# Second softmax of each head's pair in PSUM, and the first block's norms and lambda's steps rearranged

## The chip, the cores and the metric

The kernel runs on one core of one Trainium2 chip. The metric is the device time of one execution in microseconds (us). The engines are TensorE (PE), VectorE (DVE), ScalarE (ACT), GpSimd (POOL) and SyncE (SP), which here only issues DMAs and opens the layers.

## The reference

256 tokens of width 1024 pass through two layers of a first block and then two layers of a second block, all in fp32. The change touches the first block alone:

```python
h = rms_norm(x, attn_norm_g[l])
proj = h @ w_in[l]
rq, rk, rv, rg, dq, dk, dv = jnp.split(proj, split_at, axis=-1)
ret = retention_bidir(rq, rk * RET_HEAD_DIM ** -0.5, rv, lg_f, lg_b)       # 8 heads of 64
ret = rms_norm(ret, ret_norm_g[l]) * jax.nn.silu(rg)
dqn = rms_norm(dq, dq_norm_g[l]) * DIFF_HEAD_DIM ** -0.5                   # 4 heads, each a pair of 64
dkn = rms_norm(dk, dk_norm_g[l])
lam = exp(sum(lambda_q1 * lambda_k1)) - exp(sum(lambda_q2 * lambda_k2)) + lam_init
da = diff_attention(dqn, dkn, dv, lam, slopes)     # (softmax(one) - lam * softmax(two)) @ v, with ALiBi
da = rms_norm(da, diff_norm_g[l]) * (1.0 - lam_init)
x = x + concatenate([ret, da]) @ w_out[l]
h = rms_norm(x, ffn_norm_g[l])
x = x + (silu(h @ w_gate[l]) * (h @ w_up[l])) @ w_down[l]
```

The second block (convolutions, two attentions, and a feed-forward that gathers rows of a table by indirect DMA) takes some 1700 of the 2400 us and is left as it is.

## The kernel before

Tokens lie on the 128 partitions in two tiles, t = 0 and 1 (`TT` = 2). `x_res` holds the residual stream, `xn` its normed rows, and the normed rows are transposed by TensorE into four PSUM banks and then split into `hT_hi` (ScalarE, L1302) and `hT_lo` (VectorE, L1659). Every weight goes the same way: SyncE loads chunks of 128 x 1024 into three slots of `raw`, ScalarE rounds each to its high part (L1279), GpSimd subtracts to make the low part (`low_part`, L1153), and TensorE multiplies three times per product (high by high, high by low, low by high; L629 is the helper that issues every matmul). There are six slots for the split pairs. Twenty-eight chunks are used up to the attention part, eight by the out projection, and 66 by the feed-forward. Each engine runs a program in an order written out by hand, and semaphores tie them together.

A layer of the first block, as far as it matters here:

- **Start.** The layer is opened by SyncE. VectorE's `norm_x` squares and sums both tiles (L1703), lets ScalarE take both roots at once (`root`, L1265), takes the reciprocals (L1706) and scales both tiles (L1709). Behind that VectorE makes lambda's two products (L1723) and two gains (L1725, L1726), and only then `hT_lo` from the transposed rows. After it come lambda's two sums (L1731, L1733) and the exponents of retention's decays (L1738 to L1741). ScalarE empties the transposed rows, takes exps of the decays' parameters and of lambda, and then exps of `rel`, with the high parts of weights in between.
- **Groups.** TensorE makes `dq` in acc[0], acc[1] and `dk` in acc[2], acc[3] (`acc` are the first four PSUM banks; the other four rotate by a plan). ScalarE squares them, VectorE reduces (L1749), ScalarE takes the root, and VectorE writes the normed groups `dqk` (L1755, L1761). TensorE waits for `dqk_ready` between its third and its fourth pair of feature blocks, to transpose two heads (L769).
- **Attention.** Scores k = 2h and 2h + 1 are the pair of head h. `biased(k)` adds ALiBi and takes the row maxima (L1770, L1775), ScalarE's `exps(k)` works in place (L1385), and `difference(h)` takes reciprocals (L1780), times lambda (L1782), scales the second softmax (L1785) and subtracts it from the first (L1789). All of this lies in `prob`, four slots in SBUF, and `attn(h, t)`. VectorE's order is biased 0 to 3, difference 0 and 1, biased 4 to 7, decayed(0), difference(2), decayed(1), difference(3), decayed(2), decayed(3), where `decayed(p)` multiplies two heads' retention scores by the decays (L1804). TensorE makes `dv`, then `ret_out(0)`, scores, `ret_out(1)`, scores, and `ret_out(2)`, which waits for `decayed(2)`. Behind that it transposes `attn`, multiplies with `dv`, transposes `mix` (L861) and runs the out projection.
- **Before the feed-forward.** The projection comes out of TensorE in the order half 0 (tile 0, tile 1), half 1 (tile 0, tile 1), each announced by `out_full`. VectorE adds a half when both its tiles are there (L1846), and after the second half runs `norm_x` as at the start.

## Time and profile before

| | |
|---|---|
| three runs, median | 2408.61 us |
| three runs, lowest and highest | 2403.22 and 2413.67 us |
| the profiled execution | 2408.13 us, with a span of 2406.3 us |
| granted TensorE clock, mean over the span | 0.944 of full |
| busy, share of the span | PE 82%, DVE 65%, POOL 52%, ACT 28% |
| chain that ended last, by engine | DMA 38%, PE 36%, DVE 17%, issue 4%, ACT 2%, POOL 2% |
| the first block's two layers | 0 to 356 us, 358 to 706 us |

The chain follows the last instruction back to what released it, step by step, so its shares say who held the end, and busy shares do not. The DMA share is the second block's gathers. In the first block the chain is nearly all TensorE's and VectorE's.

### The profile page before, as it was taken

What the parts mean: (1) busy time and instruction counts of PE and PEld (TensorE: products, weight loads), DVE (VectorE), ACT (ScalarE), POOL (GpSimd) and SP (SyncE); (2) the same over time, 40 slices, a digit from 0 to 9 for tenths busy, and PEclk for the clock granted to TensorE, in tenths of its full rate; (3) what the DMA queues carried; (4) which work ended last, traced back from release to release, by engine and by line L of the source; (5) the groups of instructions that cost most, each with busy time, mean ns of one, the idle gap of its engine ahead of it and who ended that gap; (6) DMA issues with size and microseconds to landing.
All of it is one profiled execution on the core that took longest, in us unless ns stands there. A gap on an engine that the chain in (4) does not pass through costs nothing.

```text
span 2406.3 us, 25784 instructions
## 1 busy us (share of the span) xinstructions
PE 1978.0 (82%) x8464; PEld 1303.1 (54%) x8464; DVE 1569.0 (65%) x3650; ACT 666.9 (28%) x1231; POOL 1246.8 (52%) x828
## 2 busy tenths in 40 slices
PE   7989999989998669888777777797688887777776
PEld 6779988779987555443232222386544433232232
DVE  7732126641115759888788877666498987888776
ACT  5534436544435421211011110154221111010100
POOL 7738867648872146555444444130455554444441
PEclk9989998999999779999999999997799999999999
DMA  5425544426554159999999999651499999999996
GB/s 177 159 70 195 192 153 159 140 96 201 183 193 147 62 193 396 421 419 421 421 421 421 421 421 421 271 191 61 154 399 421 420 421 421 421 422 420 421 420 275
DMA packets 118012, 700.21 MB, mean 291 GB/s; under 512 B 13968, under 2 KB 13968, under 8 KB 51856
## 3 DMA queue, kind: packets, MB, share of 16 engines
q0 software_dynamic: 73728, 536.90, 53.9%
q1 hardware_dynamic: 44176, 161.96, 19.7%
q8 instruction: 56, 0.92, 0.2%
q14 instruction: 52, 0.43, 0.1%
HBM read 697.76 MB, written 1.05 MB: 290 GB/s over the span
## 4 chain that ended last, share of the span: by engine, by line
DMA 38%; PE 36%; DVE 17%; issue 4%; ACT 2%; POOL 2%; SPq 0%; DVEq 0%; POOLq 0%; ACTq 0%
PE ps L629 35%; DMA arena<-in_table,arena 18%; DMA late_row<-in_table,arena 18%; DVE arena L2203 3%; POOL w_split L1153 2%; DVE late_row L2203 1%; DVE diag L2213 1%; DMA row_sb<-in_table,arena 1%; DVE arena L1925 1%; DVE arena L1789 1%; DVE arena L1785 1%; ACT arena L1471 1%; POOL arena L1239 1%; ACT w_split L1279 1%; DVE arena L1723 0%
## 5 line engine op out<-in xcount | busy, mean ns | idle before, releaser
L1153 POOL TENSOR_TENSOR w_split<-raw,w_split 128x1024 fp32r<-128x1024 f32 x260 | 636.5, 2469 | 399.4 <-ACT w_split L1279 397.6
L629 PE MATMUL ps<-late_row,diag 128*128 128x512 f32 x1000 | 472.0, 615 | 120.4 <-DVE diag L2213 120.4
L629 PE MATMUL ps<-arena,diag 128*128 128x512 f32 x888 | 431.6, 630 | 133.3 <-DVE diag L2213 133.3
L629 PE MATMUL ps<-hT_hi,w_split 128*128 128x256 f32 x2624 | 503.4, 290 | 28.5 <-POOL w_split L1153 23.9
L629 PEld LDWEIGHTS ps<-hT_hi,w_split 128*128 128x128 f32 x2624 | 419.6, 193 | 38.6 <-issue 27.2
L1239 POOL DMA_INDIRECT late_row<-in_table,arena x250 | 285.2, 1141 | 298.1 <-PE ps L629 277.9
L1239 POOL DMA_INDIRECT arena<-in_table,arena x222 | 253.0, 1140 | 324.7 <-PE ps L629 268.4
L629 PEld LDWEIGHTS ps<-late_row,diag 128*128 128x128 f32 x1000 | 185.8, 194 | 396.6 <-DVE diag L2213 206.5
L629 PE MATMUL ps<-hT_lo,w_split 128*128 128x256 f32 x1312 | 374.4, 285 | 0.0
L629 PEld LDWEIGHTS ps<-arena,diag 128*128 128x128 f32 x888 | 167.5, 198 | 380.1 <-DVE diag L2213 210.1
L2203 DVE CUSTOM_DVE_ANT_0 late_row<-late_row,x_res 128x1024 f32<-128x1024 f32 x250 | 307.4, 1235 | 98.1 <-DMA late_row<-in_table,arena 98.1
L1565 ACT ACTIVATE arena<-arena 128x2 f32<-128x2 f32 x260 | 52.9, 203 | 1120.6 <-DVE arena L2203 1120.6
L1279 ACT ACTIVATE w_split<-raw 128x1024 fp32r<-128x1024 f32 x288 | 300.6, 1057 | 195.9 <-DMA raw<-in_stream 140.5
L2203 DVE CUSTOM_DVE_ANT_0 arena<-arena,x_res 128x1024 f32<-128x1024 f32 x222 | 277.0, 1254 | 90.6 <-DMA arena<-in_table,arena 90.1
L629 PEld LDWEIGHTS ps<-hT_lo,w_split 128*128 128x128 f32 x1312 | 253.8, 193 | 7.2 <-issue 5.3
L629 PE MATMUL ps<-w_split,hT_hi 128*128 128x512 f32 x640 | 211.7, 414 | 20.5 <-DVE hT_lo L1659 6.0
L1673 DVE TENSOR_TENSOR arena<-arena,ps 128x256 f32<-128x256 f32 x44 | 18.6, 422 | 290.9 <-ACT arena L1329 290.9
L2213 DVE TENSOR_SCALAR diag<-ident,arena 128x128 f32<-128x128 f32 x512 | 175.3, 400 | 22.6 <-ACT arena L1565 16.3
L629 PEld LDWEIGHTS ps<-w_split,hT_hi 128*128 128x128 f32 x640 | 125.7, 200 | 52.0 <-issue 11.8
L629 PE MATMUL ps<-w_split,hT_lo 128*128 128x512 f32 x320 | 130.0, 406 | 0.0
L629 PE MATMUL ps<-arena 128*128 128x64 f32 (+7 forms) x632 | 108.6, 354 | 24.5 <-ACT arena L1313 13.0
L629 PEld LDWEIGHTS ps<-arena 128*128 128x128 f32 (+2 forms) x632 | 94.1, 227 | 41.6 <-ACT arena L1313 15.2
(241 smaller groups left out, 1914.9 us busy)
## 6 DMA issues: line engine op xcount, KB each, us to landing
raw<-in_stream SPq DMA_DIRECT2D x288, 512.0 KB, 3.3
row_sb<-in_row SPq DMA_DIRECT2D x2, 2306.5 KB, 11.2
late_row<-in_table,arena POOLq DMA_INDIRECT x250, 30.1
arena<-in_table,arena POOLq DMA_INDIRECT x222, 29.1
arena<-in_sub SPq DMA_DIRECT2D x2, 1024.0 KB, 11.5
arena<-in_small SPq DMA_DIRECT2D x2, 640.0 KB, 8.8
x_res<-in_x SPq DMA_DIRECT2D x1, 1024.0 KB, 5.7
out_x<-x_res SPq DMA_DIRECT2D x2, 512.0 KB, 5.3
```

The lines of the kernel that those rows point to most:

```text
L629: ins = nc.tensor.matmul(o, lhsT, rhs, start=start, stop=stop)
L1153: pool.tensor_tensor(w_lo[pair], raw[:, at % raws, :], w_hi[pair].bitcast(F32), ALU.subtract).then_inc(lo_ready, 1)
L1239: pool.indirect_dma_start(out=slots[slot_of[n]], out_offset=None, in_=table, in_offset=bass.IndirectOffsetOnAxis(ap=picked[:, u, at:at + 1 ...
L1279: A(w_hi[pair_of(c, self.pairs, self.narrow)], raw[:, slot, :], ACT.Copy).then_inc(hi_ready, 1)
L1471: ins = A(prob2[:, k % 4, t, 0:n], prob2[:, k % 4, t, 0:n], ACT.Exp, bias=negmax2[:, k, t:t + 1], accum_out=sums2[:, k, t:t + 1])
L1565: A(acts[:, some], dots[:, some], ACT.Gelu).then_inc(acts_ready, 1)
L1673: V.tensor_tensor(full, value, gate, ALU.mult).then_inc(gate_step, 1)
L1785: step(V.tensor_scalar(attn(h, t), prob[:, two % 4, t, :], rsum[:, two, t:t + 1], None, ALU.mult))
L1789: V.scalar_tensor_tensor(out=attn(h, t), in0=prob[:, one % 4, t, :], scalar=rsum[:, one, t:t + 1], in1=attn(h, t), op0=ALU.mult, op1=ALU.s ...
L1925: step(V.scalar_tensor_tensor(out=dst[:, c, :], in0=x, scalar=tap, in1=dst[:, c, :], op0=ALU.mult, op1=ALU.add))
L2203: ins = V.tensor_tensor_reduce(out=x, in0=x, in1=x_res[:, n // TILE_ROWS, :], scale=1.0, scalar=0.0, op0=ALU.mult, op1=ALU.add, accum_out= ...
L2213: V.tensor_scalar(diag[:, n % DIAGS, :], ident[:], acts[:, n:n + 1], gate[:, n // TOP, n % TOP:n % TOP + 1], ALU.mult, ALU.mult).then_inc( ...
```

## The change

1. `probs(k)` stands where `prob[:, k % 4]` stood: for odd k, the second softmax of each pair, it is a PSUM bank, acc[2] for heads 0 and 2 and acc[3] for heads 1 and 3. Bias, exp, scaling and difference of odd k read and write it there, and `attn(h, t)` is written only by the last step.
2. At a layer's start tile 0's sum of squares is ScalarE's and tile 1's is VectorE's, and each tile has its own root, reciprocal and scaling.
3. Lambda's products and the two gains stand behind the decays' exponents on VectorE, lambda's exp behind the decays' exp on ScalarE, and lambda's sums behind `dqk`.
4. Before the feed-forward each tile of each half is added as it comes. The squares of half 0 are summed in advance and go, scaled and with epsilon, into the bias of the root (`eps_x`), tile 0's half 1 is squared by VectorE and tile 1's by ScalarE, and each tile has its own root.
5. ScalarE tries a root of a constant (`root_tried`) ahead of each layer's opening. Counts of `std_ready` are renumbered.

```diff
+        def probs(k):
+            return acc[2 + k // 2 % 2].rearrange("p (t c) -> p t c", t=TT) if k % 2 else prob[:, k % 4]
...
-                root(1, std_x, ss_x, 1.0 / D, eps1)
+                A(xn[:, 0, :], x_res[:, 0, :], ACT.Square, accum_out=ss_x[:, 0:1]).then_inc(act_step, 1)
+                act.wait_ge(act_step, 1)
+                root(None, std_x[:, 0:1], ss_x[:, 0:1], 1.0 / D, eps1)
+                root(1, std_x[:, 1:2], ss_x[:, 1:2], 1.0 / D, eps1)
                 w.upto(0)
                 act.wait_ge(par_ready, 32)
                 empty_transposed(B, w, "xT", col1_sb[:, 0:DT])
                 A(dece, row1_sb[:, slice(*r1["dec"])], ACT.Exp).then_inc(dec_ready, 1)
-                act.wait_ge(lam_ready, 1)
-                A(lam_e, lam_s, ACT.Exp).then_inc(lame_ready, 1)
...
                 A(decay[:, :, P:2 * P], decay[:, :, P:2 * P], ACT.Exp).then_inc(decay_ready, 1)
+                act.wait_ge(lam_ready, 1)
+                A(lam_e, lam_s, ACT.Exp).then_inc(lame_ready, 1)
...
-                        ins = A(prob[:, k % 4, m, :], prob[:, k % 4, m, :], ACT.Exp, bias=negmax[:, k, m:m + 1],
+                        ins = A(probs(k)[:, m, :], probs(k)[:, m, :], ACT.Exp, bias=negmax[:, k, m:m + 1],
...
-                root(4, std_x, ss_x, 1.0 / D, eps1)
+                act.wait_ge(ms_ready, 4)
+                A(std_x[:, 0:1], ss_x[:, 0:1], ACT.Sqrt, bias=eps_x[:, 0:1], scale=1.0 / D).then_inc(std_ready, 1)
+                act.wait_ge(ms_ready, 5)
+                A(xn[:, 1, 512:D], x_res[:, 1, 512:D], ACT.Square, accum_out=ss_x[:, 1:2]).then_inc(act_step, 1)
+                act.wait_ge(act_step, 3)
+                A(std_x[:, 1:2], ss_x[:, 1:2], ACT.Sqrt, bias=eps_x[:, 1:2], scale=1.0 / D).then_inc(std_ready, 1)
...
                 with act.Fori(0, DEPTH) as l:
+                    if n == 1:
+                        A(root_tried, eps1[:, 0:1], ACT.Sqrt)
                     enter_layer(act, "act", l + n)
...
+            def sum_of_squares(t, c, out):
+
+                x = x_res[:, t, c]
+                return V.tensor_tensor_reduce(out=xn[:, t, c], in0=x, in1=x, scale=1.0, scalar=0.0,
+                                              op0=ALU.mult, op1=ALU.add, accum_out=out)
+
+            def normed_rows(step, t, n):
+
+                dve.wait_ge(std_ready, n)
+                step(V.reciprocal(rstd_x[:, t:t + 1], std_x[:, t:t + 1]))
+                step.settle()
+                V.tensor_scalar(xn[:, t, :], x_res[:, t, :], rstd_x[:, t:t + 1], None, ALU.mult).then_inc(rows_ready, 1)
...
-                norm_x(step, 1)
-                dve.wait_ge(par_ready, 32)
...
+                step(sum_of_squares(1, slice(0, D), ss_x[:, 1:2]))
+                step.settle()
+                dve.sem_inc(ms_ready, 1)
+                for t in range(TT):
+                    normed_rows(step, t, t + 1)
                 empty_transposed(B, "xT", col1_sb[:, 0:DT])
-                dve.wait_ge(lame_ready, 1)
-                step(V.tensor_tensor(lam_d, lam_e[:, 0:1], lam_e[:, 1:2], ALU.subtract))
-                step.settle()
-                step(V.tensor_tensor(lam, lam_d, par("lam_init"), ALU.add))
...
                 dve.sem_inc(dist_ready, 1)
 
+                dve.wait_ge(par_ready, 32)
+                lq, lk = par("lq"), par("lk")
+                for m in range(2):
+                    c = slice(64 * m, 64 * m + 64)
+                    step(V.tensor_tensor_reduce(out=falling[:, 0, c], in0=lq[:, c], in1=lk[:, c], scale=1.0, scalar=0.0,
+                                                op0=ALU.mult, op1=ALU.add, accum_out=lam_s[:, m:m + 1]))
+                step(V.tensor_scalar(gq, par("dq_g"), 64 ** -0.5, None, ALU.mult))
+                step(V.tensor_scalar(gd, par("diff_g"), par("out_scale"), None, ALU.mult))
+                step.settle()
+                dve.sem_inc(lam_ready, 1)
...
                 ins.then_inc(dqk_ready, 1)
+
+                dve.wait_ge(lame_ready, 1)
+                step(V.tensor_tensor(lam_d, lam_e[:, 0:1], lam_e[:, 1:2], ALU.subtract))
+                step.settle()
+                step(V.tensor_tensor(lam, lam_d, par("lam_init"), ALU.add))
...
-                        ins = V.tensor_tensor_reduce(out=prob[:, k % 4, t, :], in0=b[:, t * SEQ:(t + 1) * SEQ],
+                        ins = V.tensor_tensor_reduce(out=probs(k)[:, t, :], in0=b[:, t * SEQ:(t + 1) * SEQ],
...
-                        step(V.tensor_scalar(attn(h, t), prob[:, two % 4, t, :], rsum[:, two, t:t + 1], None,
+                        step(V.tensor_scalar(probs(two)[:, t, :], probs(two)[:, t, :], rsum[:, two, t:t + 1], None,
                                              ALU.mult))
                     step.settle()
                     for t in range(TT):
-                        V.scalar_tensor_tensor(out=attn(h, t), in0=prob[:, one % 4, t, :],
-                                               scalar=rsum[:, one, t:t + 1], in1=attn(h, t),
+                        V.scalar_tensor_tensor(out=attn(h, t), in0=probs(one)[:, t, :],
+                                               scalar=rsum[:, one, t:t + 1], in1=probs(two)[:, t, :],
                                                op0=ALU.mult, op1=ALU.subtract).then_inc(attn_ready, 1)
...
+                def added(t, c):
+                    dve.wait_ge(out_full, 3 + TT * c + t)
+                    x = x_res[:, t, halves[c]]
+                    step(V.tensor_tensor(x, x, acc[2 * t + c], ALU.add))
+
+                for t in range(TT):
+                    added(t, 0)
+                step.settle()
+                for t in range(TT):
+                    step(sum_of_squares(t, halves[0], ss_x[:, t:t + 1]))
+                step.settle()
+                step(V.tensor_scalar(eps_x, ss_x, 1.0 / D, float(EPS1), ALU.mult, ALU.add))
+                step.settle()
+                added(0, 1)
+                step.settle()
+                step(sum_of_squares(0, halves[1], ss_x[:, 0:1]))
+                step.settle()
+                dve.sem_inc(ms_ready, 1)
+                added(1, 1)
+                step.settle()
+                dve.sem_inc(ms_ready, 1)
+                for t in range(TT):
+                    normed_rows(step, t, 6 + t)
```

## Rows read from the trace of the kernel before

**Rows 1.** Stage, first layer's attention: length; busy PE, PEld, DVE, ACT, POOL; PEclk; DMA

```profile
94.00:136.00 42.00, 36.02 (x200) 31.32 (x198) 31.08 (x51) 19.05 (x38) 22.04 (x10) 0.84 0.32 107
```

**Rows 2.** Chain of waits: start, duration, what; attention part of both layers

```profile
97.95 2.33 DVE arena L1782
100.31 4.85 DVE arena L1785 x2
...
113.13 4.94 DVE arena L1789 x2
...
136.28 8.44 PE ps L629 x36
...
486.02 8.42 PE ps L629 x36
```

**Rows 3.** Timeline, VectorE: start, duration, instruction [idle before]; attention part, first layer

```profile
81.03 0.62 DVE L1785 TENSOR_SCALAR arena<-arena 128x256 f32<-128x256 f32 x2
81.69 0.88 DVE L1789 SCALAR_TENSOR_TENSOR arena<-arena 128x256 f32<-128x256 f32 x2
...
117.99 2.73 DVE L1804 TENSOR_TENSOR arena<-ps,arena 128x256 f32<-128x256 f32 x8
```

**Rows 4.** Timeline, GpSimd, the same part

```profile
82.40 9.48 POOL L1153 TENSOR_TENSOR w_split<-raw,w_split 128x1024 fp32r<-128x1024 f32 x4 [2.03 <-ACT w_split L1279]
97.83 7.15 POOL L1153 TENSOR_TENSOR w_split<-raw,w_split 128x1024 fp32r<-128x1024 f32 x3 [5.95 <-ACT w_split L1279]
...
110.59 9.69 POOL L1153 TENSOR_TENSOR w_split<-raw,w_split 128x1024 fp32r<-128x1024 f32 x4 [0.34 <-ACT w_split L1279]
```

**Rows 5.** Timeline, TensorE, retention's matmuls of the first layer

```profile
108.68 5.96 PE L629 MATMUL ps<-arena 128*128 128x64 f32 x48
118.79 7.09 PE L629 MATMUL ps<-arena 128*128 128x64 f32 x32 [4.14 <-DVE arena L1804]
```

**Rows 6.** Timeline, ScalarE and VectorE, retention's norm of the first layer

```profile
125.92 1.09 ACT L1414 ACTIVATE arena<-ps 128x512 f32<-128x512 f32 x2 [8.21 <-PE ps L629]
...
131.48 1.29 DVE L1828 TENSOR_TENSOR arena<-arena 128x512 f32<-128x512 f32 x2
```

**Rows 7.** Timeline, VectorE, ScalarE and TensorE, start of the second layer

```profile
361.26 1.42 DVE L1709 TENSOR_SCALAR arena<-x_res,arena 128x1024 f32<-128x1024 f32 x2
...
367.73 3.23 DVE L1659 SCALAR_TENSOR_TENSOR hT_lo<-ps,col_sb,hT_hi 128x256 fp32r<-128x256 f32 x8
...
364.57 3.02 ACT L1302 ACTIVATE hT_hi<-ps,col_sb 128x256 fp32r<-128x256 f32 x8 [1.65 <-PE ps L661]
...
362.07 3.68 PE L661 MATMUL ps<-ident,arena 128*128 128x128 f32 x16 [5.95 <-DVE arena L1709]
368.75 1.19 PE L629 MATMUL ps<-w_split,hT_hi 128*128 128x512 f32 x2 [3.00 <-DVE hT_lo L1659]
```

**Rows 8.** Timeline, GpSimd, ScalarE, VectorE and TensorE, groups of the second layer

```profile
370.53 14.82 POOL L1153 TENSOR_TENSOR w_split<-raw,w_split 128x1024 fp32r<-128x1024 f32 x5 [3.34 <-ACT w_split L1279]
...
397.40 0.32 ACT L1265 ACTIVATE arena<-arena,eps 128x32 f32<-128x32 f32 x1
...
393.74 1.28 DVE L1749 TENSOR_REDUCE arena<-arena 128x8 f32<-128x512 f32 x2 [9.23 <-ACT arena L1359]
...
406.17 3.49 DVE L1761 TENSOR_TENSOR arena<-arena,row_sb 128x512 f32<-128x512 f32 x2
...
410.19 1.04 PE L769 MATMUL ps<-ident,arena 128*128 128x128 f32 x8
```

**Rows 9.** Timeline, ScalarE and TensorE, start of the first layer

```profile
8.70 1.28 ACT L1265 ACT_TABLE_LOAD   x1
...
11.53 3.67 PE L661 MATMUL ps<-ident,arena 128*128 128x128 f32 x16 [11.53 <-DVE arena L1709]
```

**Rows 10.** Timeline, VectorE and TensorE, before the first layer's feed-forward

```profile
160.57 1.23 DVE L1703 CUSTOM_DVE_ANT_0 arena<-x_res 128x1024 f32<-128x1024 f32 x1
...
164.47 3.65 PE L661 MATMUL ps<-ident,arena 128*128 128x128 f32 x16 [5.26 <-DVE arena L1709]
```

More of the change, by code:

```diff
@@ L1698, in slice_of @@
                 return slice(P - t * P, P - t * P + SEQ)
-            def norm_x(step, n):
-                for t in range(TT):
-                    step(V.tensor_tensor_reduce(out=xn[:, t, :], in0=x_res[:, t, :], in1=x_res[:, t, :], scale=1.0,
-                                                scalar=0.0, op0=ALU.mult, op1=ALU.add, accum_out=ss_x[:, t:t + 1]))
-                root_of(step, n)
-                step(V.reciprocal(rstd_x, std_x))
+            def sum_of_squares(t, c, out):
[5 more added lines that the diff above has]
+                step(V.reciprocal(rstd_x[:, t:t + 1], std_x[:, t:t + 1]))
                 step.settle()
-                for t in range(TT):
-                    V.tensor_scalar(xn[:, t, :], x_res[:, t, :], rstd_x[:, t:t + 1], None,
-                                    ALU.mult).then_inc(rows_ready, 1)
+                V.tensor_scalar(xn[:, t, :], x_res[:, t, :], rstd_x[:, t:t + 1], None, ALU.mult).then_inc(rows_ready, 1)
             def block1(l):
```

25 lines of the change are left out of this document (7 added, 18 removed).

## The prediction

> **What bounds the kernel now.** I read the chain of waits first, for the first block's two layers alone (the change touches nothing behind them). Over most of a layer it is TensorE's own matmuls; it leaves TensorE in three places, and each lies under an edit. (1) In the attention part the chain runs through VectorE's `difference`: four pairs at L1785 and L1789, the first of 4.85 us and the last of 4.94, take 15.42 us together [rows 2]. TensorE, meanwhile, ends 48 matmuls at 114.64, idles 4.14 us, and then needs 7.09 us for 32 of the same: 0.222 us each against 0.124 [rows 5]. The clock's mean there is 0.84 [rows 1], so the idle time cost the upper of the two levels (2.4 GHz) too. (2) At a layer's start TensorE waits 3.00 us for `hT_lo`, because VectorE first does lambda's products (L1723) while ScalarE's half is already there [rows 7]. (3) Between out projection and feed-forward TensorE idles 5.26 us for the whole norm [rows 10].
>
> Why is (1) so dear? The same pairs cost 0.62 and 0.88 us when GpSimd is idle (81.03 to 82.4; GpSimd resumes at 82.40 after 2.03 idle), while L1804, which reads one operand in PSUM, takes 2.73 for 8 = 0.34 each right beside a busy GpSimd (110.59 to 120.28) [rows 3, 4]. So an SBUF-only form waits for GpSimd's 2.4 us low parts; a form with a PSUM operand doesn't.
>
> **Part one: the second softmax in PSUM.** Banks acc[2] and acc[3] are free then: `dqk` has been made from them, and the out projection comes behind `difference`. L1785 becomes PSUM to PSUM and L1789 reads one operand from SBUF, one from PSUM. The trace has no VectorE or ScalarE instruction that writes PSUM, so the price is bounded: below by 0.31 (half of the 0.62 pair, uncontended SBUF), above by the contended 2.4; I take 0.40, nearest to L1804's 0.34 and the uncontended 0.44 of L1789 [rows 3]. ScalarE's exps of odd k and VectorE's bias of odd k change their target only: zero, plus or minus 0.1 each, on which TensorE waits under 1 us twice a layer.
>
> The Trainium skill, "VectorE: DVE Perf Modes", section on the perf-mode tier table, speaks against this edit: an fp32 `tensor_scalar` runs at two elements a cycle in SBUF but at one with a PSUM operand, and its cost formula gives an estimate of 0.39 us for 256 elements against 0.19. By that rule alone part one would lose some 0.2 us x 8 a layer. The same skill's "SBUF — State Buffer", section on the two separate sides, calls the port pair that VectorE shares with GpSimd an exclusive lock, held for a whole instruction; the trace agrees [rows 3, 4], and by it the edit gains.
>
> The new path, first layer. `decayed(0)` ends just before 97.95; L1782 stays SBUF to SBUF and still waits for GpSimd (2.33, to 100.3) [rows 2, 4]; then 4 x 0.4 end at 101.9. `decayed(1)` waits for the scores that TensorE makes halfway through `dv` and ends at about 104.6; L1782 waits again (up to 2.4), 4 x 0.4, end about 108.7. `decayed(2)` is asked for only at about 111, when TensorE has made its scores, so VectorE is some 2 us early and the idle goes. TensorE does the last 32 at 0.124 = 3.97: 114.64 + 3.97 = 118.6 instead of 125.88.
>
> What is late next is retention's norm: squares, reduce, a table load, a root, two multiplies. From the first square (125.92) to L1828's end (131.48 + 1.29 = 132.77) that is 6.9 us [rows 6]; from 118.6 it ends at 125.5. Transposes of `mix`, ScalarE's and VectorE's halves and their hand-overs add about 1.9: the out projection starts near 127.4, not 136.28 [rows 2]. **8.9 us.** In the second layer the same places lie 351.2 us later and the projection starts at 486.02 [rows 2], where the clock had come back sooner: 127.4 + 351.2 = 478.6, **7.5 us**. GpSimd's parts for the projection end by 120.28 [rows 4], in time. But between 118.6 and 127.4 TensorE has only some 3.6 us of work; if its clock falls there, the projection's first matmuls run at 1.2 GHz, about 2 us lost. I take off 0.5 a layer for that.
>
> **Part two: the norm before the feed-forward.** Halves 0 are added and squared while TensorE is at half 1: GpSimd is idle then, and there are 4 us of room. Tile 0 of half 1 is complete 6 matmuls (1.36 us) before tile 1. VectorE: add 0.65, square of 512 elements (half of 1.23 [rows 10]), root 0.30 on ScalarE, beside which tile 1 is added (159.4 to 160.05); reciprocal and scaling to 161.1. TensorE starts tile 0 at 161.15 instead of 164.47. Tile 1: ScalarE's square of 512 (0.6) and its accumulator, root, VectorE's scaling, to 162.3, before tile 0's eight transposes at 0.23 are through (163.0). So both tiles, and everything behind them, come 164.47 - 161.15 = 3.3 us sooner. **3.3 us a layer, 6.6 in all.** The extra [128 x 2] step and the settles stand in the idle time. If TensorE's clock survives the shorter gap, the transposes take half: 0.95 more a layer.
>
> **Part three: a layer's start.** Second layer: ScalarE squares tile 0 while VectorE squares tile 1, the Sqrt table having been loaded before the layer opens. Tile 0 is scaled to 360.8 instead of about 362.0 (361.26 + 0.71), so transposes start 1.2 sooner [rows 7]. Behind them VectorE is free: `hT_lo` follows ScalarE's first pair (now at 363.2) instead of starting at 367.73. First matmul 365.1, not 368.75: 3.65. But the third weight chunk's high part is behind ScalarE's eight empties, a table load and two small steps, and comes only about 1.45 sooner; GpSimd then makes a low part each 2.4 us plus 3.2 us once, held by the decays' three long instructions. From 370.53 (five took 14.82 [rows 8]) less 1.45, plus 6 x 2.4 + 3.2, it ends the eighth at 386.7, so the second group of matmuls (12 of 0.227 a chunk) ends at 389.4 instead of 392.9: 3.5. Then the root of the groups (high part 11 needs the raw slot that low part 8 frees) at 395.15 instead of 397.7, plus the 11.94 from the root to L1761's end (409.66): `dqk` is ready at 407.1 while TensorE arrives at 406.7. It goes on at 407.2 instead of 410.19 [rows 8]. **3.0 us.** Lambda's products behind the decays are covered by the wait for the second squares (VectorE idles 9.23 us there [rows 8]), and lambda's two sums (at most two low parts, 4.8) by the transposes and the 48 matmuls of the fourth feature pair, which stand between `dqk` and the first scores; if that cover went they would cost up to 4.8.
>
> First layer: ScalarE's new try of the root comes behind Sin's, so the table load stays at 8.70 [rows 9]; then come the try, the square and the root, to 11.65. VectorE waits: transposes start at 12.7, 1.15 later than 11.53 [rows 9]. Without lambda's products in front, the first matmul still is 1.3 sooner. But the third chunk is 0.9 later, and low part 8 with it, and the root of the groups moves back by about 0.5, which is all the slack that TensorE has on `dqk` (410.19 - 409.66 in the second layer [rows 8]). **0.1 us**, between -0.6 and +0.9.
>
> **Sum.** 8.9 + 7.5 + 6.6 + 3.0 + 0.1 = 26.1, less 1.0 for the clock: 25.1. The profiled execution took 2408.13 (span 2406.3 and 1.8 around it), practically the median of the runs, 2408.61. 2408.1 - 25.1 = **2383.0**.
>
> **The rivals.**
> A. The clock falls in the thinned stretch in both layers (4 us instead of 1), and the fronts give nothing (VectorE's scaling of tile 1 and GpSimd's first low part are due within 0.1 us of each other at about 361.0; if GpSimd wins, up to 2.4 is lost; L1761's four contended steps can also take 3 us more): 26.1 - 4.0 - 3.1 = 19.0, 2389.1. For it: the clock fell after 4.14 idle [rows 5]. Against it: it has to go wrong in both layers. 0.22.
> B. The clock stays up everywhere: 2 x 0.95 more, no loss of 1.0, and 1.0 more at the fronts: 29.0, 2379.1. 0.08.
> C. The change doesn't do what it says: with a PSUM tensor the pointer scalar `rsum` is still in SBUF, and no row has such a form of VectorE beside a busy GpSimd. Then part one gives nothing and 6.6 + 3.1 = 9.7 stay: 2398.4, within half a per cent. 0.08.
> D. Slower: each of the eight steps of heads 2 and 3 waits for a whole low part and then runs at PSUM's price, 2.4 + 0.4 = 2.8 us, on the path that sets TensorE's idle. 8 x 2.8 - 15.42 = 7.0 more a layer, 14.0, less 9.7: 2412.4. It decides from (15.42 + 4.9) / 8 = 2.54 us a step on; to be slower by 0.5% it needs 3.3. 0.04, half of it beyond 0.5%.
> The forecast has 0.58.
>
> **How the numbers follow.** Half a per cent (12 us) is about what a measurement of this kernel tells from no change. Faster by more: forecast, A and B, 0.88. Within: C and half of D, 0.10. Slower: 0.02. The range goes below B by the spread of the runs before (2403 to 2414, so 5 us) to 2374, and above A by 8 to 2397, where C begins; it leaves out C, D and thin tails.
>
> **What would show it.** Right: L1785's and L1789's successors at 0.3 to 0.5 us each with GpSimd busy; no idle over 1 us of TensorE between the `dv` group and retention's last matmul, which runs at 0.124 a piece; `hT_lo` a pair behind `hT_hi` at both starts; transposes before the feed-forward about 2 us behind the last out projection; first layer's first transposes later than 11.53. Wrong: those steps still at 1.4 to 2.8 us (C, D); a long wait on `dqk` or on low parts at the front; TensorE at 0.4 us per 512 columns at the projection's start (A).

## The result and the profile after

| | before | after |
|---|---|---|
| median of the runs | 2405.91 us (4 runs, 2394.33 to 2413.67) | 2379.76 us (4 runs, 2378.72 to 2382.35) |
| ratio, 95% interval | | 0.9904, 0.9878 to 0.9930 |
| span of the profiled execution | 2406.3 us | 2378.4 us |
| mean granted clock | 0.944 | 0.946 |

The change took 26.15 us off the medians; 25.1 were predicted. The ratio of 0.9904 is 23 us of 2405.91, and its interval reaches from 17 to 29. To see where they lie I cut each profile at the same four places of a layer: first transposes of `dqk`, first matmul of the out projection, first and last matmul of the feed-forward. The pieces, in us ("front" is from the layer's begin to `dqk`'s transposes, "attention" from there to the projection, "gap" from there to the feed-forward, "FF" the feed-forward itself, "rest" the untouched second block):

| | front | attention | gap | FF | front | attention | gap | FF | rest |
|---|---|---|---|---|---|---|---|---|---|
| before | 59.15 | 77.13 | 32.49 | 187.36 | 54.22 | 75.67 | 32.48 | 187.36 | 1700.4 |
| after | 59.10 | 68.18 | 28.61 | 187.36 | 51.02 | 68.17 | 28.50 | 189.33 | 1698.1 |
| difference | -0.05 | -8.95 | -3.88 | 0 | -3.20 | -7.50 | -3.98 | +1.97 | -2.3 |

The first block ends 25.6 us sooner, at 680.27 instead of 705.86. The rest's 2.3 us can't be put down to the change: in the nine profiles of this study with the same code there, that piece took 1693.9 to 1700.4.

**Attention.** The stage of [rows 1], 94 to 136 before, is now 94 to 127 (length; busy PE, PEld, DVE, ACT, POOL; PEclk; DMA), and the second layer's with TensorE alone:

```profile
94.00:127.00 33.00, 30.24 (x200) 25.64 (x198) 19.98 (x51) 18.81 (x38) 21.25 (x10) 1.00 0.42 138
...
429.00:462.00 33.00, 30.41 (x200) 1.00 0.41 138
```

The clock that had a mean of 0.84 is granted in full. VectorE's timeline there, for [rows 3]:

```profile
98.21 2.12 DVE L1803 TENSOR_SCALAR arena<-arena 128x2 f32<-128x2 f32 x1
100.37 0.89 DVE L1806 TENSOR_SCALAR ps<-ps,arena 128x256 f32<-128x256 f32 x2
101.29 0.87 DVE L1810 SCALAR_TENSOR_TENSOR arena<-arena,ps 128x256 f32<-128x256 f32 x2
...
105.00 1.25 DVE L1803 TENSOR_SCALAR arena<-arena 128x2 f32<-128x2 f32 x1
106.29 0.89 DVE L1806 TENSOR_SCALAR ps<-ps,arena 128x256 f32<-128x256 f32 x2
107.21 0.87 DVE L1810 SCALAR_TENSOR_TENSOR arena<-arena,ps 128x256 f32<-128x256 f32 x2
111.93 1.42 DVE L1825 TENSOR_TENSOR arena<-ps,arena 128x256 f32<-128x256 f32 x4 [3.84 <-PE ps L635]
```

L1806 and L1810 are the old L1785 and L1789. Two of each take 0.89 and 0.87 us where they took up to 4.85 and 4.94 [rows 2]. GpSimd is as busy as it was then, which its timeline shows, against [rows 4]:

```profile
97.89 7.09 POOL L1159 TENSOR_TENSOR w_split<-raw,w_split 128x1024 fp32r<-128x1024 f32 x3 [5.98 <-ACT w_split L1285]
104.93 2.55 POOL L1185 TENSOR_TENSOR arena<-arena,row_sb 128x512 f32<-128x512 f32 x2
```

The tiny step L1803 (lambda times reciprocals, 2 elements per partition) is still SBUF to SBUF and still takes 2.12 us: it ends at 100.33, when GpSimd's first low part of the row above (7.09 us for three) is through. VectorE then idles 3.84 us before `decayed(2)`, so it is early, and TensorE's idle of 4.14 [rows 5] is gone. TensorE's timeline:

```profile
108.94 9.68 PE L635 MATMUL ps<-arena 128*128 128x64 f32 x80
```

Eighty matmuls at 0.121 us in one go, where there were 48, idle time and 32 at 0.222. The chain of waits (start, length, what) runs through no VectorE work here but retention's norm:

```profile
96.66 21.97 PE ps L635 x136
...
118.66 1.08 ACT arena L1423 x2
...
127.28 2.74 PE ps L635 x11
```

**Start of a layer.** TensorE's timeline of the second layer, for [rows 7], then VectorE's and TensorE's before `dqk`'s transposes, for [rows 8]:

```profile
347.75 3.67 PE L667 MATMUL ps<-ident,arena 128*128 128x128 f32 x16 [4.52 <-DVE arena L1727]
352.14 1.19 PE L635 MATMUL ps<-w_split,hT_hi 128*128 128x512 f32 x2 [0.72 <-DVE hT_lo L1675]
...
390.10 3.51 DVE L1777 TENSOR_TENSOR arena<-arena,row_sb 128x512 f32<-128x512 f32 x2
```

The wait for `hT_lo` is 0.72 instead of 3.00. `dqk` is ready at 393.61 and TensorE comes to it at 394.27 by its own pace. In the first layer the table load stays where it was (8.65 against 8.70), the transposes start 1.02 us later than before and the first matmul 1.29 sooner. From there on the chain of waits goes through two low parts (ScalarE's and TensorE's timelines, then the chain; for [rows 9]):

```profile
8.65 1.28 ACT L1602 ACT_TABLE_LOAD   x1
...
12.55 3.67 PE L667 MATMUL ps<-ident,arena 128*128 128x128 f32 x16 [12.55 <-DVE arena L1727]
16.94 1.20 PE L635 MATMUL ps<-w_split,hT_hi 128*128 128x512 f32 x2 [0.72 <-DVE hT_lo L1675]
...
21.01 6.84 POOL w_split L1159 x2
...
27.89 31.21 PE ps L635 x204
```

**Before the feed-forward.** VectorE's and TensorE's timeline, for [rows 10]: VectorE squares and scales tile by tile, and TensorE waits 2.46 us instead of 5.26, then transposes at the upper clock (16 in 1.94 us, not 3.65).

```profile
149.69 0.69 DVE L1719 CUSTOM_DVE_ANT_0 arena<-x_res 128x512 f32<-128x512 f32 x1
150.53 0.69 DVE L1868 TENSOR_TENSOR x_res<-x_res,ps 128x512 f32<-128x512 f32 x1
151.77 0.75 DVE L1727 TENSOR_SCALAR arena<-x_res,arena 128x1024 f32<-128x1024 f32 x1 [0.24 <-DVE arena L1725]
...
152.67 1.94 PE L667 MATMUL ps<-ident,arena 128*128 128x128 f32 x16 [2.46 <-DVE arena L1727]
```

In the second layer the clock did fall there, and took 1.97 us of the feed-forward stage: 0.63 us for two matmuls at 1.2 GHz, 0.40 at 2.4 GHz.

```profile
487.63 2.64 PE L667 MATMUL ps<-ident,arena 128*128 128x128 f32 x16 [2.25 <-DVE arena L1727]
490.94 0.55 PE L635 MATMUL ps<-hT_hi,w_split 128*128 128x256 f32 x1 [0.67 <-DVE hT_lo L1675]
...
491.50 0.63 PE L635 MATMUL ps<-hT_hi,w_split 128*128 128x256 f32 x2
```

### The profile page after: what moved, and what is told of

It is laid out like the page before. It is cut to its first block, busy times and chain, and to the rows that moved or that the text cites. A ratio compares the mean times of both kernels' runs of the same rounds, so it can differ in the third digit from the quotient of the medians.

```text
span 2378.4 us, 25810 instructions
## 1 busy us (share of the span) xinstructions
PE 1973.8 (83%) x8464; PEld 1295.8 (54%) x8464; DVE 1527.1 (64%) x3656; ACT 671.6 (28%) x1245; POOL 1234.6 (52%) x828
## 3 DMA queue, kind: packets, MB, share of 16 engines
HBM read 697.76 MB, written 1.05 MB: 294 GB/s over the span
## 4 chain that ended last, share of the span: by engine, by line
PE 39%; DMA 38%; DVE 15%; issue 3%; ACT 3%; POOL 2%; DVEq 0%; SPq 0%; POOLq 0%; ACTq 0%
PE ps L635 38%; DMA late_row<-in_table,arena 21%; DMA arena<-in_table,arena 15%; DVE arena L2242 2%; DMA row_sb<-in_table,arena 2%; DVE late_row L2242 2%; DVE diag L2252 1%; POOL w_split L1159 1%; DVE arena L1964 1%; ACT arena L1485 1%; ACT w_split L1285 1%; DVE row_sb L2242 0%; PE ps L667 0%; DVE arena L2208 0%; POOL arena L1245 0%
## 5 line engine op out<-in xcount | busy, mean ns | idle before, releaser
L635 PE MATMUL ps<-arena,diag 128*128 128x512 f32 x888 | 437.4, 637 | 123.3 <-DVE diag L2252 123.2
L635 PEld LDWEIGHTS ps<-w_split,hT_hi 128*128 128x128 f32 x640 | 125.5, 201 | 43.9 <-issue 5.8
L635 PE MATMUL ps<-arena 128*128 128x64 f32 (+7 forms) x632 | 99.2, 333 | 19.9 <-ACT arena L1319 14.8
L635 PE MATMUL ps<-w_split,hidw_hi 128*128 128x512 f32 x352 | 109.4, 392 | 0.0
```

The lines of the kernel that those rows point to most:

```text
L635: ins = nc.tensor.matmul(o, lhsT, rhs, start=start, stop=stop)
```

## The experiments

The same pieces for every kernel run, in the order in which they are told. Where an experiment was timed in several runs, its ratio is to the kernel before in runs beside it: a median of 2401.04 us (27 runs) for the first four, 2402.15 (11 runs) for the last four. Each line below comes from one profile.

| | front | attention | gap | FF | front | attention | gap | FF | rest |
|---|---|---|---|---|---|---|---|---|---|
| psum_only | 60.15 | 68.17 | 32.50 | 187.35 | 53.52 | 68.23 | 32.49 | 187.35 | 1695.1 |
| norms_only | 59.12 | 76.10 | 29.69 | 187.35 | 51.03 | 76.64 | 29.44 | 187.36 | 1693.9 |
| lambda_back | 61.35 | 68.21 | 29.68 | 187.36 | 52.90 | 68.24 | 28.47 | 187.36 | 1694.3 |
| ff_norm_back | 59.00 | 68.19 | 32.49 | 189.00 | 51.06 | 68.23 | 32.47 | 189.25 | 1700.3 |
| psum_scale_only | 60.43 | 68.19 | 32.48 | 187.36 | 53.56 | 68.19 | 32.49 | 187.36 | 1695.3 |
| low_in_halves | to projection: 128.14 | | 32.51 | 187.36 | 54.06 | 67.91 | 32.53 | 187.35 | 1695.0 |
| third_early | 58.10 | 69.84 | 28.99 | 188.99 | 50.12 | 69.83 | 28.74 | 189.08 | 1695.0 |
| sin_later | 56.63 | 68.16 | 29.52 | 187.36 | 51.06 | 69.77 | 28.95 | 188.87 | 1691.5 |
| sin_later_timed | 56.87 | 69.84 | 29.21 | 187.36 | 51.98 | 68.20 | 28.45 | 187.35 | 1698.9 |
| awake | 59.13 | 68.16 | 28.55 | 187.35 | 51.09 | 68.21 | 28.50 | 187.36 | 1699.5 |
| sin_awake | 57.12 | 68.21 | 28.55 | 187.36 | 52.01 | 69.77 | 28.52 | 187.35 | 1695.5 |
| all_three | 56.03 | 68.14 | 28.54 | 187.36 | 50.43 | 68.13 | 28.50 | 187.36 | 1701.5 |

**psum_only**: the kernel before with item 1 of the change alone.

```diff
...
-                        step(V.tensor_scalar(attn(h, t), prob[:, two % 4, t, :], rsum[:, two, t:t + 1], None,
+                        step(V.tensor_scalar(probs(two)[:, t, :], probs(two)[:, t, :], rsum[:, two, t:t + 1], None,
...
-                                               scalar=rsum[:, one, t:t + 1], in1=attn(h, t),
+                                               scalar=rsum[:, one, t:t + 1], in1=probs(two)[:, t, :],
```

> Part one alone on the kernel before. Theory (SBUF-only steps of difference queue behind GpSimd's low parts, a PSUM operand lets them pass; they set TensorE's idle): scaling and subtraction at 0.4 to 0.45 us each beside a busy GpSimd, no idle before ret_out(2), out projection of the first layer starts at 127.3 instead of 136.28, 9.0 sooner, of the second layer 7.5 more; 16.5 us in all, ratio 0.993. Rival (PSUM price or pointer scalar eats it): steps at 1.4 to 2.8 us, ratio 0.999 to 1.003. Rival (the gain exists only together with the new norms): under 10 us.

Measured: 2390.93 us (10 runs), ratio 0.9964 (0.9946 to 0.9982). In the profile both attention stages are those of the changed kernel, and the first block ends 16.1 us sooner, as the theory had it. So item 1 does all of the attention part. The steps take 0.49 and 0.48 us, a little over the expected 0.45. The time missed the expectation, though: the interval of its ratio (4 to 13 us) leaves out 0.993. Why the runs show less than this profile's first block is open.

**norms_only**: the changed kernel with item 1 undone.

```diff
-            return acc[2 + k // 2 % 2].rearrange("p (t c) -> p t c", t=TT) if k % 2 else prob[:, k % 4]
+            return prob[:, k % 4]
...
```

> Everything but part one: the changed kernel with prob and attn in SBUF as before. Theory (parts add up): 0.1 + 3.1 at the two starts, 3.9 + 4.0 before the feed-forwards, less 2.0 where the clock comes back late in one feed-forward: 9 to 11 us, ratio 0.9955 to 0.9965. Rival (what is gained at the starts is lost again in VectorE's queue behind GpSimd, because difference is the bound): the out projections start at 136.3 and about 478 after the first layer's gain is taken off, total 6 to 8.

Measured: 2393.27 us (10 runs), ratio 0.9953 (0.9933 to 0.9974). The first block ends 9.1 us sooner; 16.1 + 9.1 = 25.2 against the 25.6 of both, so the two halves of the change add up. That they do so within 0.4 us is partly chance: falls of the clock of 1 to 2 us sit in different places of the three profiles. The steps of `difference` are back at their old price (VectorE's timeline):

```profile
100.29 4.84 DVE L1806 TENSOR_SCALAR arena<-arena 128x256 f32<-128x256 f32 x2
105.17 2.84 DVE L1810 SCALAR_TENSOR_TENSOR arena<-arena 128x256 f32<-128x256 f32 x2
```

**lambda_back**: the changed kernel with item 3 undone, so that lambda's products stand ahead of `hT_lo` again.

```diff
                 for t in range(TT):
                     normed_rows(step, t, t + 1)
+                for m in range(2):
+                    c = slice(64 * m, 64 * m + 64)
+                    step(V.tensor_tensor_reduce(out=falling[:, 0, c], in0=lq[:, c], in1=lk[:, c], scale=1.0, scalar=0.0,
+                                                op0=ALU.mult, op1=ALU.add, accum_out=lam_s[:, m:m + 1]))
...
                 empty_transposed(B, "xT", col1_sb[:, 0:DT])
...
```

> The changed kernel with lambda's products, sums and exp put back before the decays. Theory A (VectorE's queue ahead of hT_lo sets the start): first matmuls 2 to 3 us later in both layers, 4 to 5 us slower in all. Theory B (GpSimd's third and fourth low parts set it, whatever VectorE does): first matmuls later, but the transposes of dqk (58.94 and 394.1 in the changed kernel) move by under 1 us a layer. Mixed: first layer B, since nothing was gained there, second layer about 2.

Measured: 2383.02 us (6 runs), ratio 0.9929 (0.9906 to 0.9952). Theory A had it right: the first matmuls come 2.6 and 2.5 us later into their layers, and the fronts are 2.25 and 1.9 us longer than in the changed kernel. In the first layer that is 2.2 longer than *before* (61.35 against 59.15). Of these, 1.3 lie ahead of the first matmul (19.57 against 18.23): that is the norm with ScalarE in it (items 2 and 5). The other 0.9 lie in the 240 matmuls behind it, which take 41.78 us instead of 40.92, and TensorE waits for nobody there in either kernel. psum_only, whose front has the code of the kernel before, shows the same 0.8 and a front of 60.15. Chain and TensorE's timeline, first of the kernel before, then of psum_only:

```profile
18.23 40.92 PE ps L629 x240
22.64 0.62 PE L629 MATMUL ps<-w_split,hT_hi 128*128 128x512 f32 x2
...
18.38 41.76 PE ps L633 x240
22.36 1.05 PE L633 MATMUL ps<-w_split,hT_hi 128*128 128x512 f32 x2
```

Two matmuls of 512 columns still take 1.05 us there, 4 us after the first, as they do wherever the granted clock is 1.2 GHz (third_early below), and 0.62 in the kernel before. The granted clock itself shows 1.00 at the start of psum_only's trace, so I go by the matmuls. The same code's front can thus differ by 1 us with the moment at which the clock comes back, and a difference of fronts of 1 us says nothing of the code by itself.

**ff_norm_back**: the changed kernel with item 4 undone.

```diff
-                act.wait_ge(ms_ready, 4)
-                A(std_x[:, 0:1], ss_x[:, 0:1], ACT.Sqrt, bias=eps_x[:, 0:1], scale=1.0 / D).then_inc(std_ready, 1)
...
+                root(4, std_x, ss_x, 1.0 / D, eps1)
...
```

> The changed kernel with the old norm before the feed-forward. Theory: the gap between last projection matmul and first feed-forward matmul goes back from 5.8 to 9.6 us in both layers; the second feed-forward takes 187.4 again instead of 189.3, if its 2 us are a matter of the clock alone: 5.5 to 8 us slower, ratio to the kernel before 0.992 to 0.993. Rival (the longer feed-forward is caused by weights that come late after the shorter gap): 189.3 stays when the gap is long, or TensorE waits there for low parts.

Measured: 2390.58 us (10 runs), ratio 0.9956 (0.9942 to 0.9971). The gap is back at 32.49 and 32.47, so item 4 is worth 3.9 and 4.0 us. What I hadn't expected: the feed-forward took 189.0 and 189.25, with the long gap, and the run 10.8 us more than the changed kernel's, not 5.5 to 8. The 1.97 us that the changed kernel loses in its second feed-forward are therefore not a price of the shorter gap. Nor do weights come late: TensorE waits for no low part at the stage's head. The clock falls in the long gap of the kernel before as well, where the transposes take 3.65 us [rows 10], but there it is back when the feed-forward begins: its first matmul takes 0.38 us. Here it takes 0.55 (TensorE's timeline), and the pairs behind it 0.63 instead of 0.40:

```profile
159.68 0.55 PE L635 MATMUL ps<-hT_hi,w_split 128*128 128x256 f32 x1 [0.65 <-DVE hT_lo L1670]
...
160.25 0.63 PE L635 MATMUL ps<-hT_hi,w_split 128*128 128x256 f32 x2
```

**psum_scale_only**: the kernel before, with odd k in PSUM up to the scaling, which writes `attn` in SBUF as before, so that the subtraction stays all SBUF.

```diff
...
-                        step(V.tensor_scalar(attn(h, t), prob[:, two % 4, t, :], rsum[:, two, t:t + 1], None,
+                        step(V.tensor_scalar(attn(h, t), probs(two)[:, t, :], rsum[:, two, t:t + 1], None,
```

> The kernel before with bias, exp and scaling of odd k reading PSUM, but the scaled second softmax written to attn in SBUF and the subtraction between two SBUF operands, as before. Theory (one SBUF operand is free of GpSimd, two are not, each instruction by itself): the scaling takes 0.40 to 0.45 us each, the subtraction stays at 1.2 to 1.8 mean. TensorE's idle before ret_out(2) shrinks from 4.14 to 0 to 1.5, so the out projection starts 67.7 to 70 us after the first transposes of dqk (before 77.1, part one alone 68.2). Rival (the writes to PSUM, not the operands read, decide): the scaling stays at 1.4 and nothing is gained.

Measured: 2387.22 us in one run, beside 2397.09 of the kernel before. VectorE's and TensorE's timelines:

```profile
101.69 0.88 DVE L1789 TENSOR_SCALAR arena<-ps,arena 128x256 f32<-128x256 f32 x2
102.61 4.18 DVE L1793 SCALAR_TENSOR_TENSOR arena<-arena 128x256 f32<-128x256 f32 x2
...
109.25 0.88 DVE L1789 TENSOR_SCALAR arena<-ps,arena 128x256 f32<-128x256 f32 x2
110.16 2.04 DVE L1793 SCALAR_TENSOR_TENSOR arena<-arena 128x256 f32<-128x256 f32 x2
...
110.28 9.68 PE L633 MATMUL ps<-arena 128*128 128x64 f32 x80
```

The subtraction still waits for GpSimd (4.18 for two), VectorE has less room, and yet TensorE has no idle left and the attention stages take 68.19 in both layers. Half the edit gives the whole gain of the stage: what counts is that `decayed(2)` comes before TensorE asks for it, and beyond that faster steps buy nothing. A step that reads one of its tensors from PSUM is free of GpSimd, whether its result goes to PSUM (0.49 us) or to SBUF (0.48).

**low_in_halves**: the kernel before, nothing in PSUM, but each of GpSimd's low parts made by two instructions of 512 columns instead of one of 1024.

```diff
-                pool.tensor_tensor(w_lo[pair], raw[:, at % raws, :], w_hi[pair].bitcast(F32),
-                                   ALU.subtract).then_inc(lo_ready, 1)
+                for c0 in (0, CH // 2):
+                    c1 = slice(c0, c0 + CH // 2)
+                    ins = pool.tensor_tensor(w_lo[pair][:, c1], raw[:, at % raws, c1], w_hi[pair][:, c1].bitcast(F32),
+                                             ALU.subtract)
+                ins.then_inc(lo_ready, 1)
```

> The kernel before with every low part of the first four stages and all others made by GpSimd in two instructions of 512 columns. Theory (a VectorE step waits for the end of GpSimd's current instruction): the waits halve with the length of GpSimd's instruction; the scaling goes from 1.42 us mean to about 0.8, the subtraction from 1.75 to about 1.0, lambda's scaling from 0.90 to 0.6; difference no longer holds TensorE or holds it under 1 us. Rival (the two engines share a bandwidth): steps keep their means within 15%.

Measured: 2386.73 us in one run. The two pairs that took 4.85 and 4.94 us take 2.64 and 2.79, the two of 2.8 stay at 2.61 and 2.81 (VectorE's timeline, then GpSimd's):

```profile
100.33 2.64 DVE L1788 TENSOR_SCALAR arena<-arena 128x256 f32<-128x256 f32 x2
103.00 2.81 DVE L1792 SCALAR_TENSOR_TENSOR arena<-arena 128x256 f32<-128x256 f32 x2
...
98.97 8.00 POOL L1155 TENSOR_TENSOR w_split<-raw,w_split 128x512 fp32r<-128x512 f32 x6 [5.44 <-ACT w_split L1282]
```

A step now takes 1.10 (scaling) and 1.32 us (subtraction) in the mean, where I had expected about 0.8 and 1.0: each waits for the instruction of 1.33 us that GpSimd is in. Lambda's scaling, for which I had expected 0.6 us, did not get shorter: 1.10 us in the mean, against 0.90 before. The four pairs take 10.85 us instead of 15.42, TensorE's idle is gone here too (80 matmuls in 9.68 us), and the second attention stage takes 67.91. So the gain of part one is to be had without PSUM. That the wait follows the length of GpSimd's instruction is what the Trainium skill, "SBUF — State Buffer", section on the two separate sides, says of the shared port pair, an exclusive lock held for a whole instruction; the trace agrees.

**third_early**: the changed kernel with the third weight chunk's high part ahead of ScalarE's eight empties, so that GpSimd's third low part doesn't wait for it.

```diff
-                w.upto(0)
+                w.upto(1)
                 act.wait_ge(par_ready, 32)
```

> The changed kernel with ScalarE's third high part moved from behind the decays' parameters to in front of the transposed rows (in its 1.4 us of idle there). Theory (GpSimd's third and fourth low parts hold TensorE at the starts, 3.1 us late behind the second): GpSimd goes on without a pause, TensorE waits for no low part there, transposes of dqk come 1 to 2.5 us sooner in each layer, until dqk itself is the bound (ready 0.5 us ahead of them now). Rival (dqk or raw's loads bind at once): under 0.5 us a layer.

Measured: 2380.5 us in one run, nothing gained; the first block ends 3.4 us later than the changed kernel's. The fronts are 1.0 and 0.9 us shorter, and no wait for a low part is left. But both attention stages are 1.66 longer, and both feed-forwards now take 189.0, which in the changed kernel only the second did. In the attention stage it is the clock. TensorE's stretch 96 to 100 (length; busy; PEclk; DMA), first of this kernel:

```profile
96.00:100.00 4.00, 4.00 (x12) 0.57 0.02 6
```

and the same stretch of the changed kernel:

```profile
96.00:100.00 4.00, 3.34 (x15) 1.00 0.03 6
```

In both TensorE had stood still 0.88 us behind the last scores, for VectorE's biases, and in both the chain runs 2.9 us through VectorE there. In one the clock fell to 1.2 GHz (one matmul of 512 columns takes 0.63 us, two take 1.05), in the other it stayed. The code around the pause is the same in both; the stage lies 1 us sooner.

**sin_later** and **sin_later_timed**: the changed kernel with ScalarE's sin and cos (for the second block) computed at the second block's start. They had made it load a table ahead of the root's in the first layer.

```diff
-            act.wait_ge(angles_ready, 1)
-            A(sin_t[:], turns[:, 0], ACT.Sin).then_inc(trig_ready, 1)
-            A(cos_t[:], turns[:, 1], ACT.Sin).then_inc(trig_ready, 1)
             for n, layer, s, m in ((1, block1, hid_ready, FF_BLOCKS), (1 + DEPTH, block2, std_ready, 8)):
+                if n > 1:
+                    act.wait_ge(angles_ready, 1)
+                    A(sin_t[:], turns[:, 0], ACT.Sin).then_inc(trig_ready, 1)
+                    A(cos_t[:], turns[:, 1], ACT.Sin).then_inc(trig_ready, 1)
```

> The changed kernel with the two Sin tables of the rotary angles behind the first block instead of ahead of it. Theory (in the first layer ScalarE's tables, 8.3 to 10.0 us, hold the first root): the Sqrt table is loaded before x arrives, the first transposes start at 10.2 to 10.6 us instead of 12.55, as col1 and row1 land near 12.2 ScalarE empties from 12.7 instead of 15.05, and the transposes of dqk come about 2 us sooner than 58.94. The second layer is unchanged. Rival (GpSimd's low parts bind): under 0.7 us.

> The edit of sin_later again, timed in rounds. Theory: its gain at the front (first dqk transposes at 56.6 instead of 59.1 us) is a fixed 2.5 us, so the median is 2374.5 +/- 3 us and the ratio to the kernel before 0.987 to 0.990, about 0.002 under the changed kernel's 0.9904. Rival: the one run at 2373.6 was the lucky end of the spread, and the clock's fall behind the second biases in the second layer (1.6 us there) or the last feed-forward gives it back: median 2378 or more.

Measured: 2373.59 us in the single run, and then 2379.15 (6 runs, 2377.83 to 2386.63), ratio 0.9910 (0.9889 to 0.9932). The theory fell. The first front is shorter by 2.5 and 2.2 us in the two profiles, as expected, but in the timed one the clock fell in the first attention stage (69.84, +1.66), and in the first gap (29.21, +0.6), which took all of it back. The second front was 1.0 longer (51.98; sin_awake has 52.01). There TensorE ran at the upper clock from the first matmul on, eleven matmuls in 2.61 us instead of the changed kernel's 4.29. So it came to the third low part too soon and waited 1.84 us for it (chain of waits):

```profile
356.24 3.45 POOL w_split L1159
...
359.73 35.53 PE ps L635 x216
```

Behind that wait the clock fell: from 361.2 to 364.1 one matmul of 512 columns takes 0.63 us, and the granted clock is 0.50.

That the first block still ended 1.0 us sooner is due to its second feed-forward, where the clock stayed up. The single run's 2373.6 had the shortest second block of all (1691.5). The rival had it right. With the sin and cos there, the second block's code is no longer quite the same either.

**awake**: the changed kernel with sixteen transposes more, whose result nobody reads, where TensorE waits for the rows before the feed-forward.

```diff
                 bs = [open_bank(pe, banks, f"{name}{i}") for i in range(4)]
+                if name == "fT":
+                    for k in range(16):
+                        nc.tensor.transpose(bs[k // 4][:, (k % 4) * P:(k % 4 + 1) * P], ident[:], ident[:])
```

> The changed kernel with sixteen transposes more of the identity ahead of the feed-forward rows, into the same PSUM banks, which the rows then overwrite. TensorE idles 2.46 us there (150.2 to 152.67); sixteen transposes at 0.11 us take 1.8 of them, so they cost nothing if the clock is still up. Theory: it is the pause that lets the clock fall at the head of the feed-forward stage; then both stages take 187.4 us (second layer 189.3 in the changed kernel) and the run takes 2377.8 us, 2.0 less. Rival: the clock falls there by something other than this pause; then one of the two stages still shows 189.0 or more and the time stays at 2379.8 +/- 2.5.

Measured: 2376.0 us (4 runs, 2370.34 to 2379.65), ratio 0.9882 (0.9856 to 0.9908). Second layer, TensorE's timeline:

```profile
485.27 1.91 PE L661 MATMUL ps<-ident 128*128 128x128 f32 x16
487.59 2.13 PE L670 MATMUL ps<-ident,arena 128*128 128x128 f32 x16 [0.41 <-DVE arena L1730]
490.99 0.36 PE L635 MATMUL ps<-hT_hi,w_split 128*128 128x256 f32 x1 [1.28 <-DVE hT_lo L1678]
```

The first matmul takes 0.36 us instead of 0.55 and both feed-forwards take 187.4. One profile couldn't carry that, since the clock also stays up by itself at times, so I take gap plus FF over all profiles with the new norm. Six stages with the extra transposes (awake, sin_awake, all_three) lie between 215.86 and 215.91 us. Twelve without them (after, norms_only, lambda_back, third_early, sin_later, sin_later_timed) lie between 215.80 and 217.98, mean 216.95, and only three of them within 0.2 of the lowest. So the clock falls behind the pause, and filling it is worth 1.07 us a layer in the mean over these profiles. One reservation: the three profiles with the extra transposes were taken later and on another chip than the experiments above. The only one without them from there, sin_later_timed, had 216.57 and 215.80, so against it the worth would be 0.3. The time itself can't show 2 us: its interval overlaps that of the changed kernel.

**sin_awake** and **all_three**: the edits of sin_later and awake together, and with third_early's besides.

> sin_later and awake together. Where sin_later alone was, the attention stage of the second layer took 1.6 us more and its feed-forward stage 1.5 us more (188.87 against 187.36). Theory (the pause ahead of the rows drops the clock): the feed-forward stages are 187.4 both, the 1.6 us in the attention stage stays, and the run takes 2372 +/- 3 us. Rival: nothing of the 1.5 us comes back, 2373.6 to 2375.

> sin_awake with the third group's high part ahead of the first layer's norms (third_early). Alone third_early won 1.0 us at the first dqk transposes and sin_later 2.5, of which both take away waits for GpSimd's low parts (sin_later had 1.84 and 0.32 us of such waits left). Theory: the two are independent, transposes at 55.6 us or before, 2371 us. Rival: the high part now delays the first rows' turned and split chunks by its 1.1 us and the front is no earlier than sin_later's 56.6; 2372 to 2374.

Measured: 2374.65 us (4 runs), ratio 0.9882 (0.9853 to 0.9910), and 2373.77 us (4 runs), ratio 0.9877 (0.9853 to 0.9902). sin_awake's stages came out as its theory said, 187.4 twice and 69.77 in the second attention stage; its time of 2374.65 lies in the range of the rival too. all_three has a first front of 56.03 us (expected 55.6, the rival 56.6) and no fall of the clock in attention, gap or feed-forward in either layer:

```profile
94.00:126.00 32.00, 29.84 (x200) 1.00 0.41 132
426.00:458.00 32.00, 29.60 (x197) 1.00 0.41 133
480.00:492.00 12.00, 10.32 (x78) 1.00 0.00 0
```

Its first block ends at 674.5, 5.8 us before the changed kernel's. The two medians differ by 6.0, but they come from four runs each at different times, and the intervals of the two ratios overlap; so the time doesn't confirm it. 2373.77 us is the lowest median among the kernels timed more than once.

## Why the prediction was right, point by point

**The cause in the attention part** was right. Steps that read PSUM don't wait for GpSimd. psum_only shows it from the one side, low_in_halves from the other: a shorter GpSimd instruction shortens the wait. Rivals C and D fell with the first profile: no step of L1806 or L1810 took over 0.493 us.

**The price of a step** was 0.49 (scaling) and 0.48 (subtraction), not 0.40; two scalings in a row take 0.89 together. The estimate of 0.39 from the Trainium skill, "VectorE: DVE Perf Modes", is below both. Neither mattered: VectorE's idle before `decayed(2)` is 3.84 us where I had worked out some 2, so 0.1 a step goes into slack. psum_scale_only shows how little: with subtractions of 2.0 and 4.2 us a pair the stage is as short.

**The sum of the attention part**, 8.9 and 7.5, measured 8.95 and 7.50, because its two ends were worked out right: 32 matmuls at the upper clock, retention's last multiply ending at 125.28 (125.5), the projection at 127.28 (127.4).

**The clock's 0.5 a layer** was charged to the wrong place. Between 118.5 and 127.3 it stayed up in the changed kernel, although TensorE has little work there. It fell ahead of the second feed-forward, where I had counted the clock for the transposes alone: 1.97 us in the stage behind them. In other kernels it fell at 96 us, behind the second biases (1.6 us), which I hadn't looked at. Rival A's place was wrong. Its price per fall, 2 us, stood on no row; the runs gave 1.5 to 2.0.

**Before the feed-forward** I had 3.3 us a layer; 3.88 and 3.98 were measured. TensorE's first transpose came 2.8 sooner relative to the projection (25.39 against 28.19 us behind it), 0.5 less than worked out: VectorE's steps for tile 0 and tile 1 stand in one line, each add and square takes 0.70 where I had 0.65 and 0.62, and between the steps pass 0.13 to 0.24 us (chain of 150.53 to 152.67) that I had mostly left out. The transposes at the upper clock gave 1.08 (0.95 named as the condition). That condition held in the first layer; in the second the transposes took 2.64 us, between the two levels.

**The second layer's start** came out at 3.2 (3.0), and the first matmul 3.7 sooner (3.65). But the bound in between was not the one that I had named. I had `dqk` ready after TensorE's arrival; it was ready 0.66 us ahead of it. Waits for the third and fourth low part took 0.9 back in the second and third chunk's matmuls, and an earlier return of the clock gave 0.5. "A long wait on low parts at the front" was one of my signs of being wrong; the waits were there, but short, 0.5 us in all.

**The first layer's start** came out at 0.05 (0.1), with transposes at 12.55 (12.7) and the first matmul 1.29 sooner (1.3). All of that was lost until `dqk`, and again not at `dqk`'s root, where I had put it: `dqk` is ready at 58.44, 0.66 before TensorE asks. Counting matmuls in the two timelines, the first eleven take 4.61 us instead of 4.18, because the clock comes back later; the next 25, up to the fourth chunk, take 6.34 instead of 5.71, for they wait for the third and fourth low part, which end by 27.85; the rest loses 0.2. third_early, which moves only the low part, wins 1.0 us. The number was right within 0.05 us, but 0.4 of what it sums up is the clock's doing and was on no list of mine.

**The sum** 26.1 - 1.0 = 25.1 stands against 25.6 at the end of the first block. It comes so near because two misses of about 1.2 (gaps) and 1.0 (clock) cancel. The time came near by luck as well. I started from 2408.1, the profiled execution, while 27 runs of the same kernel have a median of 2401.04; the 26.15 between the medians are 23, between 17 and 29, by the ratio. The median of 2379.76 even lies on rival B's 2379.1, but B isn't what happened: the clock did fall.

What stays open: what makes the second block vary by 6.5 us with the same code, why the runs of psum_only show less than its profile, and why the clock falls in one of two equal pauses and not in the other, and comes back sooner in one start than in another.

## What to carry to other kernels

Before moving an operand to PSUM to get VectorE away from a busy GpSimd, ask how early it has to be: one operand of one of two steps sufficed here, and so did halving GpSimd's instructions, at no cost in PSUM banks. When a gain at the front of a stage disappears by its end, look at the granted clock and at the length of the matmuls behind each pause before looking for a new wait; two edits worth 1.0 and 2.3 us at the front were hidden by it. A pause of TensorE that can't be removed can be filled with work that nobody reads; in six stages out of six the clock then stayed up.

## What the runs showed of the hardware

- A `tensor_scalar` of 128x256 fp32 takes 0.49 us from PSUM to PSUM and 0.48 from PSUM to SBUF, beside a busy GpSimd; the same in SBUF took 0.31 with GpSimd idle [rows 3] and up to 2.4 with it busy.
- VectorE's fused bias takes 0.448 us into PSUM and 0.422 into SBUF; ScalarE's exp in place takes 0.430 in PSUM and 0.499 in SBUF:

```profile
L1791 DVE CUSTOM_DVE_ANT_0 ps<-ps,window 128x256 f32<-128x256 f32 x8 | 3.2, 448 | 0.0
L1791 DVE CUSTOM_DVE_ANT_0 arena<-ps,window 128x256 f32<-128x256 f32 x8 | 3.1, 422 | 21.7 <-PE ps L635 21.7
L1394 ACT ACTIVATE arena<-arena 128x256 f32<-128x256 f32 x8 | 4.0, 499 | 0.4 <-DVE arena L1796 0.4
L1394 ACT ACTIVATE ps<-ps,arena 128x256 f32<-128x256 f32 x8 | 3.4, 430 | 0.0
```

- A fall of the clock costs 1.5 to 2.0 us in an attention or feed-forward stage of this kernel. With the same code around it, a pause of 0.88 us was followed by a fall at 95.7 us and by none at 96.7.
